# A two-layer hybrid decoder step: from four equal token groups with two half-width matmuls per weight tile to five unequal parts with one, and norms by log and exp

## The reference, cut to what matters

```
u = rmsnorm(h) * g
layer 0:  xb, gate = u @ w_in_a                 (1024 -> 2 x 1024)
          xc = causal depthwise conv of width 4 over xb
          r, i = sigmoid(block-diagonal products of xc, 8 blocks of 128 x 128)
          a = exp(-8 r softplus(-lambda)); b = sqrt(1 - a*a) * (i * xc)
          h_t = a_t h_(t-1) + b_t                (a scan over tokens)
          y = (h * silu(gate)) @ w_out_a
layer 1:  q, k, v, gate = u @ w_in_b            (1024 -> 1024, 256, 256, 1024)
          attention over the last 128 keys, 16 heads on 4 key heads, ALiBi, one learned sink per head
          y = (o * silu(gate)) @ w_out_b
each:     h = h + y
          h = h + sigmoid(rmsnorm(h) @ w_ple_gate) * (p @ w_ple_proj)
end:      rmsnorm(h) * final_g, and the new states and caches
```

## Time and profile before

| | |
|---|---|
| median of 3 runs | 2182.64 us (2178.88 to 2183.03) |
| profiled execution | 2187.79 us, of which the span from first to last instruction is 2186.0 us |
| mean granted clock of PE | 0.960 |
| PE, PEld busy | 2045.8 us (94%), 1959.9 us (90%) |
| DVE, ACT, POOL busy | 1179.6 us (54%), 913.8 us (42%), 627.7 us (29%) |
| DMA | 386.46 MB, mean 177 GB/s |

### The profile page before, as it was taken

How to read it: one execution, slowest core, us unless ns; L and a number is a source line. 1 busy time by engine, 2 the same in 40 slices (tenths; PEclk the granted TensorE clock), 3 DMA queues, 4 the chain that set the end, 5 groups by cost and what they waited for, 6 DMA issues and landing times.

```text
span 2186.0 us, 40782 instructions
## 1 busy us (share of the span) xinstructions
PE 2045.8 (94%) x16454; PEld 1959.9 (90%) x16454; DVE 1179.6 (54%) x2257; ACT 913.8 (42%) x1704; POOL 627.7 (29%) x476
## 2 busy tenths in 40 slices
PE   6889999889999999989989999998998999998996
PEld 5789999688999999878989999987998999997896
DVE  7883515864388331583448533177345934238634
ACT  5664434554356221463326531155234633126432
POOL 5356652345612111022211211112230221112222
PEclk8999999899999999999999999989999999999998
DMA  6476784236746455214444645511463654541245
GB/s 262 145 280 252 258 307 170 88 121 230 279 153 233 161 198 207 104 59 155 167 173 166 234 162 215 184 59 59 164 223 139 222 187 166 209 145 59 99 170 208
DMA packets 87249, 386.46 MB, mean 177 GB/s; under 512 B 10768, under 2 KB 34704, under 8 KB 50704
## 3 DMA queue, kind: packets, MB, share of 16 engines
q1 hardware_dynamic: 87056, 383.77, 48.9%
HBM read 294.69 MB, written 89.05 MB: 176 GB/s over the span
## 4 chain that ended last, share of the span: by engine, by line
PE 72%; DVE 16%; issue 4%; ACT 3%; POOL 3%; DMA 2%; SPq 0%; DVEq 0%; ACTq 0%; POOLq 0%
PE psum L1137 62%; DVE conv_out L861 3%; PE psum L1213 3%; DVE scores L951 2%; PE psum L1225 2%; PE psum L1174 2%; DVE inv_rms L839 1%; DVE scores L934 1%; POOL w L511 1%; DVE row_max L923 1%; DMA w<-w_big_split 1%; DVE lru_or_o L885 1%; POOL square_sum_in L520 1%; PE psum L1260 1%; PE psum L1261 1%
## 5 line engine op out<-in xcount | busy, mean ns | idle before, releaser
L1137 PE MATMUL psum<-b_hi,w 128*128 128x260 f32 x4608 | 785.1, 289 | 13.2 <-DMA w<-w_big_split 7.9
L1137 PE MATMUL psum<-a_hi,w 128*128 128x260 f32 x4096 | 693.5, 288 | 19.3 <-DVE conv_in L853 6.1
L1137 PEld LDWEIGHTS psum<-b_hi,w 128*128 128x128 f32 x4608 | 655.5, 193 | 17.6 <-issue 9.7
L1137 PEld LDWEIGHTS psum<-a_hi,w 128*128 128x128 f32 x4096 | 580.1, 191 | 27.0 <-issue 16.4
L1137 PE MATMUL psum<-b_lo,w 128*128 128x260 f32 x2304 | 471.2, 287 | 0.0
L1137 PE MATMUL psum<-a_lo,w 128*128 128x260 f32 x2048 | 417.6, 286 | 9.3 <-issue 9.3
L1137 PEld LDWEIGHTS psum<-b_lo,w 128*128 128x128 f32 x2304 | 363.3, 193 | 0.0
L1137 PEld LDWEIGHTS psum<-a_lo,w 128*128 128x128 f32 x2048 | 321.2, 192 | 9.9 <-issue 9.9
L520 POOL TENSOR_TENSOR square_sum<-square_sum,square 128x520 f32<-128x520 f32 x112 | 148.9, 1330 | 461.5 <-ACT square L636 461.5
L511 POOL TENSOR_TENSOR w<-w_stage,w 128x1024 fp32r<-128x1024 f32 x68 | 168.4, 2477 | 179.7 <-ACT w L629 179.6
L636 ACT ACTIVATE square<-resid 128x520 f32<-128x520 f32 x112 | 71.5, 638 | 270.5 <-DVE resid L1021 190.7
(11 more groups left out here) (159 smaller groups left out, 2681.4 us busy)
## 6 DMA issues: line engine op xcount, KB each, us to landing
w<-w_big_split SPq DMA_DIRECT2D x207, 1024.0 KB, 4.9
w_big_split<-w SPq DMA_DIRECT2D x68, 1024.0 KB, 6.7
w_stage<-w_big SPq DMA_DIRECT2D x68, 512.0 KB, 5.4
w<-w_small_split SPq DMA_DIRECT2D x48, 256.0 KB, 4.1
y_out<-resid SPq DMA_DIRECT2D x4, 2080.0 KB, 7.3
resid<-x SPq DMA_DIRECT2D x4, 2080.0 KB, 10.7
x_stage<-x SPq DMA_DIRECT2D x32, 260.0 KB, 5.0
p_stage<-p SPq DMA_DIRECT2D x8, 520.0 KB, 6.8
```

The lines of the kernel that those rows point to most:

```text
L1137: ins = nc.tensor.matmul(PSUM[:, 2 * p + a, 0:C], W[:, s, w, k, :], x[:, k, a * C:(a + 1) * C], start=(k == 0 and n == 0), stop=(k == nk - ...
```

## The change

1. The 2080 tokens become five parts: part 0 has the first 512 prompt tokens and no sample tokens; parts 1 to 4 have 384 prompt tokens and 8 sample tokens each, together 392. Each weight tile is multiplied once, with 512 or 392 columns, in one PSUM bank. The pass over all weights is done five times instead of four.
2. Banks 0 to 3 take the big blocks in turn, banks 6 and 7 the P and p blocks in turn; the gate products of even and odd tiles use banks 4, 5 and 6, 7.
3. `root` takes a logarithm and then exp(-0.5 x) on ACT; the table that has both is loaded ahead of the wait for the sum. `inverse` becomes a wait; DVE computes no reciprocal of a norm.
4. Attention has 16 units in part 0 and 12 in each other part, with 3 and 4 input tiles of g blocks in each unit. What belongs to sample tokens is left out in part 0, as are the final norm, the y store and the second x load, for which there is no part before.
5. All five parts are written out; there is no loop. Where a part's tokens cross a border of the arrays in HBM, and for its sample tokens, transfers of x, p and y are cut into pieces.

```diff
+class Part:
+    def __init__(self, n, first, blocks, group):
+        self.samples = group is not None
+        self.tp = blocks * BLK
+        self.t = self.tp + TS * self.samples
+        self.flat = self.s0 + SG * SEG if self.samples else self.tp
+        self.nu = blocks * NKV
...
+        self.pieces = []
+        b = first
+        while b < first + blocks:
+            run = min(first + blocks - b, 4 - b % 4)
+            self.pieces.append((b // 4, b % 4 * BLK, run * BLK, (b - first) * BLK))
+            b += run
+        if self.samples:
+            self.pieces.append((group, TP, TS, self.tp))
+        self.fill = (KT - 2) * KT // self.nu
...
+PARTS = [Part(0, 0, 4, None)] + [Part(1 + i, 4 + 3 * i, 3, i) for i in range(GROUPS)]
+MAIN = 4
+BANK = [6 + ORDER[c][1] % 2 if is_small(c) else SIZE_INDEX[c] % MAIN for c in range(NBLK)]
...
                     for n, (w, x) in enumerate(((0, hi_t), (0, lo_t), (1, hi_t))):
-                        for a in range(2):
-                            ins = nc.tensor.matmul(PSUM[:, 2 * p + a, 0:C], W[:, s, w, k, :], x[:, k, a * C:(a + 1) * C],
-                                                   start=(k == 0 and n == 0), stop=(k == nk - 1 and n == 2))
+                        ins = nc.tensor.matmul(PSUM[:, BANK[c], 0:p.t], W[:, c % RING, w, k, :], x[:, k, 0:p.t],
+                                               start=(k == 0 and n == 0), stop=(k == nk - 1 and n == 2))
...
-            def root(g, n, banks, dst):
-                act.wait_ge(ms_done.sem, ms_done.at(g, n + 1))
-                nc.scalar.activation(halves(dst), PSUM[:, banks:banks + 2, 0:C], ACT.Sqrt, scale=1.0 / D,
-                                     bias=EPT[:, 0:1]).then_inc(root_done.sem, 1)
+            def root(n, o, bank, dst, load=True):
+                if load:
+                    nc.scalar.preload_act_table_set("natural_log_exp_and_others")
+                act.wait_ge(ms_done.sem, ms_done.at(n, norm_no(n, o)))
+                t = dst.shape[1]
+                link(nc.scalar.activation(dst, PSUM[:, bank, 0:t], ACT.Ln, scale=1.0 / D, bias=EPT[:, 0:1]))
+                nc.scalar.activation(dst, dst, ACT.Exp, scale=-0.5).then_inc(root_done.sem, 1)
...
-            def inverse(g, n, dst):
-                dve.wait_ge(root_done.sem, root_done.at(g, n + 1))
-                link(g, v.reciprocal(dst, dst))
+            def inverse(n, o):
+                dve.wait_ge(root_done.sem, root_done.at(n, norm_no(n, o)))
...
-                else:
-                    pe.wait_ge(ri_read.sem, ri_read.at(g, n))
+                if n > 1:
+                    pe.wait_ge(ri_read.sem, ri_read.at(g, n - 1))
                 for w in range(2):
-                    for a in range(2):
-                        ins = nc.tensor.matmul(PSUM[:, 4 + 2 * w + a, 0:hw], WRI[:, w * KT + n, :],
-                                               XC[:, n % 2, a * hw:(a + 1) * hw], start=True, stop=True)
+                    ins = nc.tensor.matmul(PSUM[:, 4 + n % 2 * 2 + w, 0:f], WRI[:, w * KT + n, :], XC[:, n % 2, 0:f],
+                                           start=True, stop=True)
...
-                sp.dma_start(XS[:, k % 2, :], group_of(A["x"], g + 1)[:, k, :]).then_inc(x_in[k % 2].sem, 16)
+                for i, c0, n, d0 in p.pieces:
+                    sp.dma_start(XS[:, k % 2, d0:d0 + n], A["x"][i][:, k, c0:c0 + n]).then_inc(x_in[k % 2].sem, 16)
...
-            group(0)
-            with pe.Fori(1, GROUPS) as g:
-                group(g)
+            for p in PARTS:
+                part(p)
```

More of the change, by code:

```diff
@@ L418, in _, with part @@
                 load_weights(j)
-            def group(g):
+            def part(p):
+                g = p.n
                 kept_up_to = 0
@@ L803, in group @@
[L803 to L814 removed]
+                        attend(p)
@@ L817, in _ @@
+            for p in PARTS:
+                part(p)
+            root(NP, "fin", 6, R[:, 0:PARTS[LAST].t])
         @block.vector
@@ L1111, in _, with project @@
-            chain[0] = 0
-            dve.wait_ge(root_done.sem, root_done.at(GROUPS, 1))
-            link(GROUPS, v.reciprocal(R[:], R[:]))
+                        attend(p)
+            for p in PARTS:
+                part(p)
+            inverse(NP, "fin")
             for k in range(KT):
-                final(GROUPS, k)
+                final(PARTS[LAST], k)
         @block.tensor
         def _(pe):
-            def project(g, c, hi_t, lo_t, ready, k0=0, k1=None):
+            def project(p, c, hi_t, lo_t, ready, k0=0, k1=None):
+                g = p.n
@@ L1353, in _ @@
-            group(0)
-            with pe.Fori(1, GROUPS) as g:
-                group(g)
-            final_sum(GROUPS)
+                        attend(p)
+            for p in PARTS:
+                part(p)
+            final_sum(PARTS[LAST])
 def kernel(**inputs):
```

1107 lines of the change are left out of this document (555 added, 552 removed).

## The result

The changed kernel takes **2128.38 us** (median of 4 runs, 2125.95 to 2133.68), the kernel before took 2182.84 beside it (2178.88 to 2190.14): a ratio of 0.975, 95% interval 0.9719 to 0.9782. The forecast was 2050. The time is inside the range (2018 to 2135), but the gain is 54 us where 132 was forecast. The profiled execution's span is 2126.6 us.

A forecast was written before the change was run, and what follows sets the result against it. PE was taken to bound five stretches, nearly z/p, with DVE pacing attention. PE-bound stages 1062, X/G 480, attention 498 and tail 14 made a 2054 us span, taken as a 2050 median; range 2018 to 2135.

The forecast's parts named there:

- I take 166 and 216: Weight products: one matmul of 392 columns was to cost 166 ns, one of 512 columns 216 ns.
- the 28: Weight products before: 260 columns took 120.1 ns, 288 cycles, 28 more than columns; claimed to be no fixed price.
- the next matmul waits for it: Weight products before: the next 128x128 weight load was said to end just after the 260 columns, holding the next matmul.
- the 8 us a part: PE-bound stages, parts 1 to 4: 8 us left for the rest beside 191.2 of weight products, making 199 a part.
- Rival 1: Matmuls outside attention: the per-matmul price stays, first form 175/225 ns, 9 ns more each, giving 2119 us; chance 0.12.
- About the same 2 us is lost: First z block: PE's wait for weight loads behind x loads was to cost about 2 us still, counted in the 8.
- 86 was forecast: X/G, parts 1 to 4: 86 us each, from 74.5 of PE work, the old 6.4 and 5 more.
- The rival at 104: X/G becomes a chain of DVE, ACT and queued DMAs, 104 a part instead of 86: +72, 2122 us; chance 0.12.
- +3 was forecast: Attention over all parts: 495 before, 498 after, no gain because DVE sets the pace.
- -4: Norms: only the last reciprocal at the kernel's end counted, tail from 18.1 to 14 us.
- Rival 4: Norms: log and exp don't share a table; extra loads for 24 norms add at most 62, 2112 us; chance 0.03.
- rival 3: Weight loads are the bound outside attention and the change makes the kernel slower, 2271 us; chance 0.05.

The follow-up runs named there:

- run 10: Changed kernel with weight products taking weights' upper 16 bits as bfloat16 and a constant contiguous bfloat16 tile as moving data: 2070.55 us, 0.9477 of the kernel before.
- run 3: Changed kernel with the norms as before (square root on ACT, reciprocal on DVE): 2160.17 us, 0.9886 of the kernel before.
- run 7: Changed kernel with the next part's first two x tiles prepared ahead of the norm at the start of z/p: 2114.44 us, 0.9683 of the kernel before.
- run 11: Changed kernel with the edits of run 7 and run 10 together: 2052.70 us, 0.9407 of the kernel before.
- run 6: Changed kernel with its large blocks turning over two PSUM banks instead of four: 2130.03 us, 0.9751 of the kernel before.
- run 4: Kernel before with only its norms changed to logarithm and exp: 2153.67 us, 0.9854 of the kernel before.
- run 1: Changed kernel followed by eleven streams of 64 matmuls: float32r steps 226.7 ns at 512 columns, 177.4 at 392, 118.8 at 260, 111.7 at 196.
- run 5: Changed kernel followed by streams of more lengths, 64 rows and other types: at 256 columns 119.9 ns in float32r, 109.3 in bfloat16.

## Why the prediction was wrong

**The step that failed** is the price of a matmul: "I take 166 and 216, because the gate products are the row in which a load is certainly covered." The gate products are the wrong row, since they are of another type. They are float32, two records to a matmul, each two cycles a column and 2.5 ns; the weight products are float32r, one record of one cycle a column and 10 to 17 ns on top. They measured 177 and 227. The sentence "So the 28 is no fixed price of a matmul" was carried from the one type to the other. And "the next matmul waits for it", the weight load as the cause of the 28 cycles at 260 columns, does not hold: the floor is 111 ns, below the 118.8 that 260 columns take in a stream, and at 392 columns, where the load should long be covered, the price on top is no smaller. That loads and matmuls both start 0.12 apart in the earlier trace rows is a common pace; it does not say which waits for which.

In numbers: 4 x 1152 x 11.4 + 1152 x 10.7 = 65 us of the 75 by which the third row of the table missed. Run 10, where the products run at 166 and 216, is 58 us faster, 50 of it in these stages. The other 10 are the 8 us a part that the prediction left for all that is no matmul there: with 1152 products at 177.4 taken off, parts 1 to 4 have 10.4, 10.2, 12.2 and 8.1, where the kernel before had 10.3. They are in z/p and O.

Rival 1, in its first form (28 cycles kept, 175 and 225, 2119 us), had the right term and lies 9 us from the time; I gave it 0.12 and should have given it the larger part, since the only rows of the same type stood for it and only a row of another type against. As a count of cycles it is not right either: at the granted clock of 0.50 nothing is paid on top (below).

The Trainium skill's page "TensorE: Matmul & The Clock Gate" (section "Back-to-back issue gap") has the form that I took, N/2.4 + 2.5 ns, as the gap of a matmul in isolation; for a stream with weight loads it gives about 81 ns at 128 columns and 131 at 512, which no stream here shows. The contiguous bfloat16 streams agree with the isolated form to 0.2 ns, from 55.8 at 128 columns to 215.8 at 512; float32r doesn't (177.4 at 392, 226.7 at 512).

**z/p and O.** "About the same 2 us is lost" was 4.6 to 6.6 in parts 1 to 3, against z/p of part 4 (43.07 us), and the prediction had itself read 4.7 in the kernel before. It left out the low clock after the wait. The shorter norm did help, which the prediction didn't count: with the old one (run 3) z/p is 2.4 and 2.6 us longer in parts 1 and 2, though not in part 3. Moving the x tiles ahead of it gave 14 us (run 7); at the forecast's price it gave 18 (runs 10 and 11). O was forecast as bound by PE, as it was before (46.1 us, o 46.2); now it is 1.5 us longer than o in parts 1 to 3 and 3.8 in part 4, by the waits for POOL shown in run 10. With the price and z/p's wait taken away the time comes to the forecast (run 11); O's waits are still in it, and attention's gain makes up for them.

**X/G.** 86 was forecast, 87.3 is the mean of parts 1 to 4. The number was right and its terms were not: PE's work is 4.4 us more than the 74.5 taken (384 x 11.4), and what stands beside it 8.4 instead of 11.4. At the forecast's price (run 10) the mean is still 85.2. Part 0 is 141.4 from the start, with 136 forecast (its terms add up to 135); the 6.8 taken off there for two reciprocals did not come, since run 3, which has them, needs 141.7. The rival at 104 did not come; run 6 shows that the four banks are not the reason.

**Attention.** 94 was forecast for a part, 90.8 measured; 122 for part 0, 121.2 measured. The matmuls gave nothing there, as said: in the runs with faster ones it did not fall (488 in run 11). But +3 was forecast, and 498 became 485; of these 13 us the norms have 7 (492 in run 3).

**Norms and tail.** The norms gave -32 in either kernel (runs 3 and 4). As terms of their own the prediction has -4 for them, in the tail, and the 6.8 of part 0; in X/G's 86 a part they are only in DVE's busy time, which isn't in the sum. So they gave more than was counted, which hid some of the partition's miss. From run 3 to after X/G fell by 13 us, z/p by 8, g by 7, the tail by 2, O and Z/P by 3. From the last weight product to the end there are 13.3 us, 14 were forecast. Rival 4 (tables) fell; ACT's table loads ahead of the norms, logarithms and exponentials in after (count, busy us, mean ns, idle before) show 21 loads for 25 norms (the prediction has 24), and none between the two passes, whose idle time is 0.6 us in all:

```profile
L650 ACT ACT_TABLE_LOAD x21 | 26.9, 1283 | 0.4
...
L653 ACT ACTIVATE inv_rms<-psum,eps 128x392 f32<-128x392 f32 (+1 forms) x20 | 12.2, 608 | 55.8 <-PE psum L1164 40.7 <-PE psum L1170 15.1
L654 ACT ACTIVATE inv_rms<-inv_rms 128x392 f32<-128x392 f32 (+1 forms) x20 | 11.0, 552 | 0.6
```

**Weight loads.** Right to count nothing: in k/v they ran at 318 GB/s and a DMA share of 0.84 with PE busy throughout (table of part 2), so rival 3 fell. In part 2 PE waits for a weight load only once, in z/p, where SP issues it late.

**What stays open:** why float32r pays its 10 to 17 ns. At 392 columns 6.5 of it go with a step of four bytes in the moving data, as bfloat16 shows; what the other 5 are no run tells, nor why the sum wanders between 10 and 17 with the length. One more fact of the trace narrows it: at the granted clock of 0.50 the products of after take 326.7 ns for 392 columns and 426.7 for 512, their columns at 1.2 GHz and nothing on top (the timeline in run 7 shows some of them). So what is paid on top appears at 2.4 GHz alone.

## What to carry to other kernels

Price a matmul from rows of the same type and the same layout of the moving data; a row of another type gives a formula that fits the eye and not the kernel. Before the gain of fewer, longer matmuls is counted, run a stream of each length behind the kernel's end: 64 of them take some 10 us and settle it. When a busy engine gets faster, look at who issues its next loads, and behind what. And compare a forecast stage by stage: a total can come out by errors that offset each other, as in run 11.

## What the runs showed of the hardware that I had not expected

- A float32r matmul of 240 to 512 columns takes its columns at 2.4 GHz and 10 to 17 ns (runs 1 and 5); from 128 to 224 columns it takes 111 to 112 ns whatever its length. At 392 columns the bank, half the weight columns, half the rows, and weights or data that stay the same change nothing (177.3 to 177.8).
- At the granted clock of 0.50 it takes its columns at 1.2 GHz and nothing on top (326.7 at 392). One wait of 2.80 us in z/p was followed by nine matmuls at that clock.
- A bfloat16 matmul takes its columns and 2.6 ns when the moving data is contiguous (166.0 at 392), 9.2 ns when each second element is taken (172.5; 12.3 at 512 columns, 225.6); a step in the weights is free (165.8). No floor shows down to 29.2 ns at 64 columns.
- High and low parts in bfloat16 therefore gain twice, at the price of fewer bits: 11.4 ns a matmul of 392 columns, and loads of 3.3 us instead of 4.9.
